# Delta rule's key and query norms in four column groups, and both windowed attentions in a new order with the band mask in the bias product

## The chip, the cores and the metric

The kernel runs on one core of a Trainium2 chip, as one launch. Its five engines (TensorE, VectorE, ScalarE, GpSimd, and SyncE for transfers) each run an instruction stream of their own and wait for one another on semaphores. The metric is the device time of a launch in microseconds.

## The reference

Two transformer blocks of different kinds follow each other, at a width of 1024, for 256 tokens (and 256 context tokens in the first block). Everything is float32. The first block has two layers, a gated delta rule mixer and a windowed attention; the second has, side by side, a convolution, a state space branch and another windowed attention, then a cross attention and an MLP. What the change touches, cut:

```python
def _l2_normalize(x):                       # first layer: queries and keys, 8 heads of 128
    return x * lax.rsqrt(jnp.sum(x * x, axis=-1, keepdims=True) + EPS)
qkv = jax.nn.silu(_short_conv(h @ w_in[:, :3072], conv_w))      # 512 tokens, 24 tiles of 128 channels
...
def _sink_softmax(logits, sink):            # both attentions: a further logit without a value
    return softmax(concatenate([sink, logits], -1), -1)[..., 1:]
# first attention: 16 heads of 64, 4 for keys and values; 256 queries;
# 512 keys (256 of the context, 256 latent ones within +-128), masked with a window
p = _sink_softmax(concatenate([q @ kc.T, where(allowed, q @ kb.T, -inf)], -1), sink)
ox = p[..., :256] @ vc + p[..., 256:] @ vb
...
# second attention: 16 heads of 64; each block of 128 queries sees its own and the previous 128 keys
bias = rel_table[bucket[dist]]              # by distance, 32 buckets, one value per head
logits = where((dist >= 0) & (dist < 128), q @ k.T * 64 ** -0.5 + bias, -1e30)
...
h = causal_depthwise_conv(a * sigmoid(gate), w, b)              # second block, 31 taps, 1024 channels
```

## The kernel before

The order of the work is written out by hand: each engine has a program, a sequence of calls such as `delta_pe`, `window_heads_dve` or `feed_pool`, and steps are named. `k.AC.after(st, "sq", m)` is the semaphore and the count at which ScalarE has done step `sq` number m of stage `st`; `mark` counts it. Nothing is reordered afterwards.

**Weights.** All weights come as one stream of 554 units of eight 128x128 tiles (512 KB) through SyncE's queue. ScalarE rounds a unit to `weights_hi` (L214), GpSimd writes the remainder `weights_lo` (L224), and each product is three matmuls (L231 to L233), high by low, low by high and high by high. Most of TensorE's work is this; it runs weights as the stationary operand (8 tiles in depth) against 256 or 512 tokens.

**Delta projection** (`delta_pe` L649, `delta_act`, `delta_dve` L755). 33 tiles of 128 channels by 512 tokens go through `linear`: tile 0 holds the gates, tiles 1 to 24 q, k and v, tiles 25 to 32 z. `linear` calls `beside(n)` behind tile n, which places small matmuls between the tiles. For each q and k tile, VectorE does the short convolution from the bank (L743 and after), ScalarE the silu and a square into `k.sq`, and TensorE, behind tiles 3 to 18, sums the square over its 128 channels: four matmuls with the square as the stationary operand (128 tokens each) and one moving column of ones, into bank 4, columns 4m to 4m+3. When the sixteen sums are there ScalarE takes the root of 128x64 (L728) and VectorE the reciprocal (L786). Behind tiles 25 to 32 TensorE spreads two of the sixteen tiles' inverse norms over all partitions, each in four transposes of a broadcast column (L688), into banks 5 and 6, and VectorE multiplies q and k by them (L790).

**Windowed attention heads** (`window_heads_pe` L1533, `_act` L1576, `_dve` L1604), the same three functions for both attentions. A step n has two heads (hh) of two blocks of 128 queries (b), so four combinations x = 2b + hh. The first attention has 512 keys for all of them, the second 128 for b = 0 and 256 for b = 1. Per step TensorE does the four score products (banks 0 to 3), then, for the step before, transposes of the probabilities in turns with the outputs (L1544 and L1555): `turned(1)`, `output(0)`, `turned(2)`, `output(1)` and so on. An output is a chain of matmuls over the key tiles with 64 columns of v as the stationary operand. The two heads go to the two halves of the output's partitions, so hh selects one of two column halves of TensorE. VectorE adds the mask and takes the maximum with one custom instruction (L1621; ahead of it a memset of a column, and behind it a negation of the maximum), ScalarE takes the exponential with its sum, VectorE adds the sink's part (L1633), takes the reciprocal and multiplies (L1640), and ScalarE copies the transposed probabilities to `swa_pt` or `attn_pt` (L1585).

**Mask and bias of the second attention.** `rel_table` (32 buckets x 16 heads) times `bucket` (32 x 384 distances) gives the bias by distance (`band_pe`); it goes to DRAM and comes back skewed into `biasm`, 128 x 16 x 256. GpSimd then adds the band mask `band` to it in four additions of 1024 columns (`band_pool` L1762). In GpSimd's program they stand between the last unit of the first attention's query weights and its output's weights.

**Convolution.** `long_conv` (L1675) is a generator of single taps on VectorE; `take(conv, n)` does n of them. Channel tiles 0 to 3 are done before the second attention's projection, tile 4 (`CONV_APART`) within its heads, four taps per step in SBUF, and tiles 5 to 7 behind them. The others accumulate in banks 6 and 7, which the heads use for outputs.

## Time and profile before

| | |
|---|---|
| median of three runs | 2959.94 us (2954.56, 2959.94, 2963.52) |
| profiled execution | 2956.96 us, of it 2955.0 us span |
| granted clock of TensorE, mean | 0.981 of full speed |
| TensorE matmul | 2811.4 us busy, 95% of the span, 21638 instructions |
| TensorE weight load | 2427.7 us, 82% |
| GpSimd | 1543.2 us, 52% |
| VectorE | 1540.9 us, 52% |
| ScalarE | 1186.2 us, 40% |
| chain that ended last | TensorE 82%, VectorE 8%, GpSimd 3%, ScalarE 3%, issue 2%, DMA 1% |

Busy time is the union of the instructions' intervals on an engine. The chain is followed back from the last instruction to what released each one, so its shares tell which engine the end of the program hung on, and where. The difference between the execution's time and its span, 1.96 us, lies outside the profiled instructions. The page gives averages over the whole program; the changed code lies in three stretches of it, and what these look like is read from the trace.

### The profile page before, as it was taken

Reading aid. Unit: us, or ns where it says so; the run is one execution under the profiler, and the core shown is the slowest. Engines: PE = TensorE matmul, PEld = TensorE weight load, DVE = VectorE, ACT = ScalarE, POOL = GpSimd, SP = SyncE. Lnnn points to the kernel's source line nnn. Section 1 sums busy time; section 2 is a strip of 40 time slices with the busy share of each in tenths; the row PEclk is TensorE's granted clock in tenths of the full one; section 3 lists DMA queues with packets and bytes.
Section 4 is the critical chain, followed back from the end, with each engine's and each line's share of the span. In section 5 each row is a group of like instructions: output and inputs, shape, how many; then the busy total and the mean of one; then the engine's idle time right before and its main releaser. Section 6 shows DMA issues by size and latency. Waiting matters only on the chain.

```text
span 2955.0 us, 52281 instructions
## 1 busy us (share of the span) xinstructions
PE 2811.4 (95%) x21638; PEld 2427.7 (82%) x21638; DVE 1540.9 (52%) x2922; ACT 1186.2 (40%) x2076; POOL 1543.2 (52%) x861
## 2 busy tenths in 40 slices
PE   7999999988889999999999998999998998998999
PEld 5888878877777788887888885799997898997999
DVE  4777235535554667316665136554284865723570
ACT  4222234324453322223222244544445465544553
POOL 4444453343324544444444452388884565696697
PEclk9999999999999999999999998999998999999999
DMA  6555322210001555324554225155553343354365
GB/s 256 203 198 200 99 76 82 89 58 3 4 3 51 174 176 178 128 93 144 178 182 156 93 89 100 57 195 190 173 186 101 109 142 108 108 164 136 116 199 164
DMA packets 106123, 381.05 MB, mean 129 GB/s; under 512 B 11392, under 2 KB 16800, under 8 KB 104608
## 3 DMA queue, kind: packets, MB, share of 16 engines
q1 hardware_dynamic: 87456, 310.60, 32.2%
q10 hardware_dynamic: 18432, 67.12, 6.5%
q8 instruction: 172, 2.82, 0.4%
q14 instruction: 63, 0.52, 0.1%
HBM read 373.47 MB, written 4.19 MB: 128 GB/s over the span
## 4 chain that ended last, share of the span: by engine, by line
PE 82%; DVE 8%; POOL 3%; ACT 3%; issue 2%; DMA 1%; SPq 0%; ACTq 0%; DVEq 0%
PE bank L231 23%; PE bank L232 22%; PE bank L233 22%; POOL weights_lo L224 2%; PE bank L822 2%; DVE norm_work L504 1%; PE upper_banks L1555 1%; DVE norm_work L498 1%; PE upper_banks L231 1%; PE upper_banks L232 1%; PE upper_banks L233 1%; DMA ada_first<-w_ada 1%; DVE square_sums L451 1%; PE bank L919 1%; PE upper_banks L838 1%
## 5 line engine op out<-in xcount | busy, mean ns | idle before, releaser
L224 POOL TENSOR_TENSOR weights_lo<-weights_landing,weights_hi 128x1024 fp32r<-128x1024 f32 x554 | 1338.5, 2423 | 1101.0 <-ACT weights_hi L214 1100.4
L214 ACT ACTIVATE weights_hi<-weights_landing 128x1024 fp32r<-128x1024 f32 x554 | 586.5, 1061 | 1235.2 <-PE bank L233 1112.7
L231 PE MATMUL bank<-normed_hi,weights_lo 128*128 128x512 f32 (+1 forms) x2664 | 912.2, 342 | 17.6 <-POOL normed_lo L520 11.9
L232 PE MATMUL bank<-normed_lo,weights_hi 128*128 128x512 f32 (+1 forms) x2664 | 900.9, 338 | 0.0
L233 PE MATMUL bank<-normed_hi,weights_hi 128*128 128x512 f32 (+1 forms) x2664 | 900.0, 338 | 0.0
L231 PEld LDWEIGHTS bank<-normed_hi,weights_lo 128*128 128x128 f32 x2664 | 502.3, 189 | 95.2 <-POOL normed_lo L520 27.6
L233 PEld LDWEIGHTS bank<-normed_hi,weights_hi 128*128 128x128 f32 x2664 | 502.1, 188 | 61.6
L232 PEld LDWEIGHTS bank<-normed_lo,weights_hi 128*128 128x128 f32 x2664 | 502.6, 189 | 58.4
L231 PE MATMUL bank<-hidden_hi,weights_lo 128*128 128x512 f32 (+1 forms) x960 | 329.1, 343 | 0.0
L232 PE MATMUL bank<-hidden_lo,weights_hi 128*128 128x512 f32 (+1 forms) x960 | 329.1, 343 | 0.0
L233 PE MATMUL bank<-hidden_hi,weights_hi 128*128 128x512 f32 (+1 forms) x960 | 329.1, 343 | 0.0
L572 DVE TENSOR_TENSOR hidden_lo<-silus,hidden_hi 128x512 fp32r<-128x512 f32 (+1 forms) x88 | 210.9, 2397 | 87.3 <-ACT hidden_hi L559 87.3
L625 DVE SCALAR_TENSOR_TENSOR residual<-bank,gate,residual 128x256 f32<-128x256 f32 x80 | 35.5, 479 | 358.3 <-PE bank L233 358.3
L231 PEld LDWEIGHTS bank<-hidden_hi,weights_lo 128*128 128x128 f32 x960 | 180.1, 188 | 24.3
L232 PEld LDWEIGHTS bank<-hidden_lo,weights_hi 128*128 128x128 f32 x960 | 180.1, 188 | 24.2
L233 PEld LDWEIGHTS bank<-hidden_hi,weights_hi 128*128 128x128 f32 x960 | 180.1, 188 | 24.2
L390 DVE CUSTOM_DVE_ANT_0 ada_products<-ada_rows,upper_banks,k_cond_pack 128x1024 f32<-128x1024 f32 x128 | 163.3, 1276 | 22.9 <-DMA ada_rows<-w_ada_rows 14.0
L390 DVE CUSTOM_DVE_ANT_0 ada_rows<-ada_rows,upper_banks,k_cond_pack 128x1024 f32<-128x1024 f32 x128 | 163.1, 1274 | 0.0
L570 DVE TENSOR_TENSOR silus<-silus,bank 128x512 f32<-128x512 f32 (+1 forms) x88 | 54.7, 621 | 183.7 <-PE bank L233 158.7
L520 POOL TENSOR_TENSOR normed_lo<-norm_work,normed_hi 128x512 fp32r<-128x512 f32 (+1 forms) x72 | 76.6, 1068 | 75.1 <-DVE norm_work L504 75.1
L1689 DVE SCALAR_TENSOR_TENSOR upper_banks<-gl,k_pack,upper_banks 128x255 f32<-128x255 f32 (+14 forms) x210 | 99.3, 473 | 7.4
L451 DVE TENSOR_TENSOR square_sums<-square_sums,squares 128x512 f32<-128x512 f32 (+1 forms) x48 | 67.3, 1402 | 35.9 <-ACT squares L443 35.9
(447 smaller groups left out, 3912.1 us busy)
## 6 DMA issues: line engine op xcount, KB each, us to landing
weights_landing<-w_up SPq DMA_DIRECT2D x176, 512.0 KB, 3.5
ada_rows<-w_ada_rows ACTq DMA_DIRECT2D x128, 512.0 KB, 4.3
weights_landing<-w_down SPq DMA_DIRECT2D x88, 512.0 KB, 3.4
weights_landing<-w_dn SPq DMA_DIRECT2D x33, 512.0 KB, 3.4
weights_landing<-w_mlp_up SPq DMA_DIRECT2D x32, 512.0 KB, 3.4
weights_landing<-w_mlp_down SPq DMA_DIRECT2D x32, 512.0 KB, 3.5
weights_landing<-w_gate SPq DMA_DIRECT2D x24, 512.0 KB, 3.4
weights_landing<-w_xbc SPq DMA_DIRECT2D x24, 512.0 KB, 3.5
```

The costliest lines, as they stand in the source:

```text
L214: k.nc.scalar.activation(k.WH[:, u % SLOTS, :], k.W[:, u % LANDS, :], ACT.Copy).then_inc(*k.AC.mark(("unit hi", u)))
L224: k.nc.gpsimd.tensor_tensor(k.WL[:, u % SLOTS, :], k.W[:, u % LANDS, :], k.WH[:, u % SLOTS, :].bitcast(F32), ALU.subtract).then_inc(*k.PO. ...
L231: nc.tensor.matmul(out, ll, rh, start=start, stop=False, skip_group_check=True)
L232: nc.tensor.matmul(out, lh, rl, start=False, stop=False, skip_group_check=True)
L233: return nc.tensor.matmul(out, lh, rh, start=False, stop=stop, skip_group_check=True)
L390: nc.vector.tensor_tensor_reduce(k.row[r % ROW_LANDS][:] if c else k.row_out[:], k.row[r % ROW_LANDS][:], k.upper[:, c * D:(c + 1) * D], 1 ...
L451: k.nc.vector.tensor_tensor(s, s, k.sq[:, d % 2, 0:tokens], ALU.add).then_inc(*k.DV.mark((st, "sum", d)))
L520: k.nc.gpsimd.tensor_tensor(lo(d), work(d), hi(d).bitcast(F32), ALU.subtract).then_inc(*k.PO.mark((st, "lo", d)))
L570: nc.vector.tensor_tensor(s, s, k.B[(2 * p + 1) % 4][:, 0:tokens], ALU.mult).then_inc(*k.DV.mark((st, "raw", p)))
L572: nc.vector.tensor_tensor(lo(p), s, hi(p).bitcast(F32), ALU.subtract).then_inc(*k.DV.mark((st, "lo", p)))
L822: mm = k.nc.tensor.matmul(bank[block(to), at + c * BLK:at + (c + 1) * BLK], lhs(rows, to, c), rhs(rows, to, c), start=True, stop=True)
L1689: nc.vector.scalar_tensor_tensor(y[:, a:LAT], x[:, 0:LAT - a], w[:, at, j:j + 1], y[:, a:LAT], ALU.mult, ALU.add).then_inc(*k.DV.mark(("co ...
```

## The change

**Norms of the delta rule.** ScalarE writes the squares of four tiles into `sq4`. Behind tiles 6, 10, 14 and 18 TensorE sums four of them at once: four matmuls with 32 columns of ones as the stationary operand and 512 moving columns, one into each group of 32 output partitions (`block(j)`) of bank 4. ScalarE copies the bank to `norms`, and later takes four roots of 512 columns; VectorE takes four reciprocals of 512. The inverse norms now lie along the columns, so a spread is one matmul with 32 rows of the identity, and behind tiles 28 to 31 four of these go to banks 4 to 7. VectorE multiplies four q or k tiles per spread group.

**Heads.** The three functions are rewritten for both attentions. TensorE takes a block's two heads together: transposes of both, then scores of a later step, then the outputs, in which the two heads alternate from matmul to matmul. The maximum is taken as a minimum of the negated values (scale -1.0, with the sink negated once), so the memset and the negation are gone, and the exponential has scale -1.0. VectorE takes the first two maxima of step n+1 ahead of and between the multiplications of step n.

**Mask.** The mask is a 33rd row of `bucket` with a row of ones in `rel_table`; GpSimd's additions and the transfer of `band` are gone. VectorE waits for the skewed transfer itself.

**Convolution.** Tile 4 is now done during the second attention's projection, three taps per step and two at the last ones, in bank 7, and is copied out like the others.

```diff
     def beside(n):
-        m = n - 3
-        if 0 <= m < 16:
-            pe.wait_ge(*k.AC.after(st, "sq", m))
-            for c in range(CHUNKS):
-                mm = nc.tensor.matmul(k.B[4][:, m * 4 + c:m * 4 + c + 1], k.sq[:, m % 2, c * P:(c + 1) * P], k.C["ones"][:, 0:1],
...
+        g = (n - 6) // 4
+        if n >= 6 and n % 4 == 2 and g < 4:
+            pe.wait_ge(*k.AC.after(st, "sq", 4 * g + 3))
+            if g:
+                pe.wait_ge(*k.AC.after(st, "norms", g - 1))
+            for j in range(4):
+                mm = nc.tensor.matmul(k.B[4][block(j), :], k.C["ones"][:, 0:BLK], k.sq4[:, j, :], start=True, stop=True)
...
-        if n > QKV:
...
-                for c in range(CHUNKS):
-                    mm = nc.tensor.transpose(ck(k.B[bank], c), column(k.rr, m * 4 + c).to_broadcast([P, P]), k.C["ident"])
+        g = n - QKV - 4
+        if 0 <= g < 4:
+            pe.wait_ge(*k.DV.after(st, "r", g))
+            if g:
+                pe.wait_ge(*k.DV.after(st, "normed", 4 * g - 1))
+            for j in range(4):
+                pick = k.C["ident"][block(j), j * BLK:j * BLK + 1].to_broadcast([BLK, P])
+                mm = nc.tensor.matmul(k.B[4 + j][:], pick, k.norms[block(j), g, :], start=True, stop=True)
...
+            if m >= 7 and m % 4 == 3 and m < 20:
+                act.wait_ge(*k.PE.after(st, "stat", m // 4 - 1))
+                nc.scalar.activation(k.norms[:, m // 4 - 1, :], B[4][:], ACT.Copy).then_inc(*k.AC.mark((st, "norms", m // 4 - 1)))
...
+                for g in range(4):
+                    nc.scalar.activation(k.norms[:, g, :], k.norms[:, g, :], ACT.Sqrt, bias=k.C["eps"]).then_inc(*k.AC.mark((st, "rms", g)))
...
+            for g in range(4):
+                dve.wait_ge(*k.AC.after(st, "rms", g))
+                nc.vector.reciprocal(k.norms[:, g, :], k.norms[:, g, :]).then_inc(*k.DV.mark((st, "r", g)))
...
-    def output(n, x):
...
         for t in range(kt):
-            mm = nc.tensor.matmul(half(k.B[6 + n % 2], hh)[:, blk(b)], w.v[:, a // P + t, at:at + HEAD], w.pt[:, x, blk(t)],
+            for hh in range(2):
+                at = (2 * (n // 4) + hh) * HEAD
+                mm = nc.tensor.matmul(half(k.B[6 + n % 2], hh)[:, blk(b)], w.v[:, a // P + t, at:at + HEAD], w.pt[:, 2 * b + hh, blk(t)],
...
+    for n in range(KT):
+        turned(n, 0)
+        turned(n, 1)
+        scores(n + 1, 1)
+        outputs(n, 0)
+        turned(n, 2)
+        turned(n, 3)
+        scores(n + 2, 0)
+        outputs(n, 1)
...
-                nc.vector.memset(w.cols[:, p, 7, x:x + 1], 0.0).then_inc(*k.DV.mark((st, "scored", n, x)))
...
-                nc.vector.tensor_scalar(nm[p][:, x:x + 1], mx[p][:, x:x + 1], -1.0, None, ALU.mult).then_inc(*k.DV.mark((st, "nm", n, x)))
...
+        maximum(n, 2)
+        maximum(n, 3)
...
+        maximum(n + 1, 0)
...
+        share(n, 0)
+        share(n, 1)
+        maximum(n + 1, 1)
+        share(n, 2)
+        share(n, 3)
...
-def band_pool(k, pool):
-    pool.wait_ge(k.skewed, 32)
...
-    window_project_dve(k, dve, attn)
-    dve.wait_ge(*k.PO.after("band", "masked", 3))
-    window_heads_dve(k, dve, attn, band_mask(k), lambda n: take(conv, 4))
+    window_project_dve(k, dve, attn, lambda n: take(conv, 3 if n < KT + 2 else 2))
+    dve.wait_ge(k.skewed, 32)
+    window_heads_dve(k, dve, attn, band_mask(k))
...
-    t["late_bucket"] = (np.arange(32)[:, None] == bucket[None, :]).astype(f)
+    t["late_bucket"] = np.concatenate([(np.arange(32)[:, None] == bucket[None, :]).astype(f), band[None, :]])
```

On TensorE's queue, one step of the first attention's heads, before (L1566 is a score, L1544 a transpose, L1555 an output matmul; in the sizes 64x128 means that 64 output partitions are written, and x4 that four of the kind follow one another):

```order
L1566 MATMUL bank<-swa_k,swa_q 128x512 x4
L1544 MATMUL upper_banks<-k_cond_pack,swa_scores 128x128 x8
L1555 MATMUL upper_banks<-swa_pt,swa_v 64x128 x4
L1544 MATMUL upper_banks<-k_cond_pack,swa_scores 128x128 x4
L1555 MATMUL upper_banks<-swa_pt,swa_v 64x128 x4
L1544 MATMUL upper_banks<-k_cond_pack,swa_scores 128x128 x4
L1555 MATMUL upper_banks<-swa_pt,swa_v 64x128 x8
```

and after (L1564 is the transpose, L1555 now the score, L1579 the output):

```order
L1564 MATMUL upper_banks<-k_cond_pack,swa_scores 128x128 x8
L1555 MATMUL bank<-swa_k,swa_q 128x512 x2
L1579 MATMUL upper_banks<-swa_pt,swa_v 64x128 x8
L1564 MATMUL upper_banks<-k_cond_pack,swa_scores 128x128 x8
L1555 MATMUL bank<-swa_k,swa_q 128x512 x2
L1579 MATMUL upper_banks<-swa_pt,swa_v 64x128 x8
```

The scores now stand in pairs between the transposes and the outputs of another step, and the outputs come in eights, whose matmuls alternate between the column halves.

On VectorE's queue, from the last statistics of the second attention's projection to its first maximum, before (L1485 is the reciprocal of a norm, L1489 the normalising, L1620 the memset, L1621 the maximum and its read, L1625 the negation):

```order
L1485 RECIPROCAL rr<-rms 128x4
L1489 SCALAR_TENSOR_TENSOR attn_q<-attn_q,k_pack,upper_banks 128x256 x2
L1620 MEMSET attn_cols 128x1
L1621 ISA attn_scores,attn_cols<-bank,biasm,k_pack 128x128
L1621 ISA attn_cols 128x1
```

and after (L1746 is a tap of the convolution, L1750 its copy):

```order
L1491 RECIPROCAL rr<-rms 128x4
L1495 SCALAR_TENSOR_TENSOR attn_q<-attn_q,k_pack,upper_banks 128x256
L1746 SCALAR_TENSOR_TENSOR upper_banks<-gl,k_pack,upper_banks 128x232
L1746 SCALAR_TENSOR_TENSOR upper_banks<-gl,k_pack,upper_banks 128x231
L1746 SCALAR_TENSOR_TENSOR upper_banks<-gl,k_pack,upper_banks 128x230
L1495 SCALAR_TENSOR_TENSOR attn_q<-attn_q,k_pack,upper_banks 128x256
L1746 SCALAR_TENSOR_TENSOR upper_banks<-gl,k_pack,upper_banks 128x229
L1746 SCALAR_TENSOR_TENSOR upper_banks<-gl,k_pack,upper_banks 128x228
L1746 SCALAR_TENSOR_TENSOR upper_banks<-gl,k_pack,upper_banks 128x227
L1746 SCALAR_TENSOR_TENSOR upper_banks<-gl,k_pack,upper_banks 128x226
L1750 COPY cv<-upper_banks 128x256
L1659 ISA attn_scores,attn_cols<-bank,biasm,k_pack 128x128
```

The taps of channel tile 4 now stand around the last two normalisings and ahead of the first maximum, where there were none.

## Rows read from the trace of the kernel before

A row of the timeline is the start in us, the busy time of the group in us, engine, line, operation, output, inputs, sizes and count, and in brackets the idle time ahead of it with what ended it. PE is TensorE, PEld its weight load, DVE VectorE, ACT ScalarE, POOL GpSimd. A row of busy time by stretch is start and end in us, the length, then the busy time (and the instructions) of PE, PEld, DVE, ACT and POOL, the granted clock, the share of the DMA engines and GB/s.

**Rows 1.** Busy time by stretch; columns named ahead.
```profile
434.00:640.00 206.00, 202.72 (x984) 166.27 (x984) 103.76 (x151) 80.52 (x104) 82.80 (x38) 1.00 0.27 88
2262.00:2316.00 54.00, 41.78 (x227) 25.80 (x226) 46.96 (x226) 27.52 (x112) 0.00 (x0) 0.81 0.03 11
```

**Rows 2.** Timeline, VectorE, first tap of three tiles, 545 to 560 us.
```profile
545.82 0.75 DVE L743 TENSOR_SCALAR dn_convs<-bank,k_pack 128x512 f32<-128x512 f32 x1 [2.61 <-PE bank L233]
552.31 0.75 DVE L743 TENSOR_SCALAR dn_convs<-bank,k_pack 128x512 f32<-128x512 f32 x1 [2.61 <-PE bank L233]
557.91 0.75 DVE L743 TENSOR_SCALAR dn_convs<-bank,k_pack 128x512 f32<-128x512 f32 x1 [1.72 <-PE bank L233]
```

**Rows 3.** Timeline, end of the delta projection, 585 to 640 us.
```profile
587.13 1.09 PE L688 MATMUL upper_banks<-k_cond_pack,rr 128*128 128x128 f32 x8 [1.26 <-DVE rr L786]
...
613.71 1.29 DVE L790 SCALAR_TENSOR_TENSOR dn_qkv<-dn_qkv,upper_banks 128x512 f32<-128x512 f32 x2 [5.19 <-PE upper_banks L688]
620.18 1.29 DVE L790 SCALAR_TENSOR_TENSOR dn_qkv<-dn_qkv,upper_banks 128x512 f32<-128x512 f32 x2 [5.19 <-PE upper_banks L688]
```

**Rows 4.** Timeline, TensorE's column groups, and VectorE's 64-column reciprocal.
```profile
24.58 1.07 PE L297 MATMUL upper_banks<-ada_first,cond 128*32 128x256 f32 x16
...
586.52 0.55 DVE L786 RECIPROCAL rr<-rms 128x64 f32<-128x64 f32 x1 [2.33 <-ACT rms L728]
...
1783.54 0.42 PEld L1356 LDWEIGHTS upper_banks<-k_cond_pack,rr 128*64 128x64 f32 x8
```

**Rows 5.** Timeline, VectorE, the sums of pairs 0, 1, 2 and 7.
```profile
1800.69 0.16 DVE L1633 TENSOR_TENSOR swa_cols<-swa_cols 128x4 f32<-128x4 f32 x1 [0.78 <-ACT swa_cols L1596]
...
1809.50 0.16 DVE L1633 TENSOR_TENSOR swa_cols<-swa_cols 128x4 f32<-128x4 f32 x1 [3.06 <-ACT swa_cols L1596]
...
1817.99 0.17 DVE L1633 TENSOR_TENSOR swa_cols<-swa_cols 128x4 f32<-128x4 f32 x1 [1.17 <-ACT swa_cols L1596]
...
1868.72 0.16 DVE L1633 TENSOR_TENSOR swa_cols<-swa_cols 128x4 f32<-128x4 f32 x1 [1.16 <-ACT swa_cols L1596]
```

**Rows 6.** Timeline, GpSimd and VectorE, 1825 to 1838 us.
```profile
1825.95 9.61 POOL L1765 TENSOR_TENSOR biasm<-biasm,band 128x1024 f32<-128x1024 f32 x4 [39.10 <-DMA biasm<-skew]
1828.57 7.68 DVE L1640 TENSOR_SCALAR swa_scores<-swa_scores,swa_cols 128x512 f32<-128x512 f32 x4
```

**Rows 7.** Timeline, first attention's heads, pair 0 and pair 7.
```profile
1801.10 1.68 DVE L1640 TENSOR_SCALAR swa_scores<-swa_scores,swa_cols 128x512 f32<-128x512 f32 x4
...
1862.08 1.99 PE L1566 MATMUL bank<-swa_k,swa_q 64*128 64x512 f32 x8
...
1863.25 0.75 DVE L1621 CUSTOM_DVE_ANT_0 swa_scores<-bank,window,k_pack 128x512 f32<-128x512 f32 x1 [0.92 <-issue]
...
1864.22 0.72 ACT L1593 ACTIVATE swa_scores<-swa_scores,swa_cols 128x512 f32<-128x512 f32 x1 [1.65 <-DVE swa_cols L1620]
...
1864.94 0.58 ACT L1585 ACTIVATE swa_pt<-upper_banks 128x512 f32<-128x512 f32 x1
...
1865.57 0.85 PEld L1555 LDWEIGHTS upper_banks<-swa_pt,swa_v 128*64 128x64 f32 x8 [0.72 <-ACT swa_pt L1585]
...
1866.59 0.66 PE L1544 MATMUL upper_banks<-k_cond_pack,swa_scores 128*128 128x128 f32 x4
```

**Rows 8.** Timeline, VectorE and TensorE, second attention's heads.
```profile
2259.61 0.18 DVE L1485 RECIPROCAL rr<-rms 128x4 f32<-128x4 f32 x1 [3.38 <-ACT rms L1453]
...
2263.05 0.35 DVE L1621 CUSTOM_DVE_ANT_0 attn_scores<-bank,biasm,k_pack 128x128 f32<-128x128 f32 x1
...
2267.27 0.15 DVE L1633 TENSOR_TENSOR attn_cols<-attn_cols 128x4 f32<-128x4 f32 x1
...
2302.55 1.94 DVE L1689 SCALAR_TENSOR_TENSOR cv<-gl,k_pack,cv 128x232 f32<-128x232 f32 x4
...
2309.98 0.16 DVE L1633 TENSOR_TENSOR attn_cols<-attn_cols 128x4 f32<-128x4 f32 x1
...
2314.01 0.39 PE L231 MATMUL bank<-normed_hi,weights_lo 128*128 128x256 f32 x1
```

223 lines of the change are left out of this document (118 added, 105 removed).

## Prediction

> **What bounds the kernel now.** The profiled execution has a span of 2955.0 us and took 2956.96 us; the median of the three runs, 2959.94 us, is 2.98 us above it, within their own spread of 9 us. I read the page first (TensorE 95% busy and 82% of the chain that ended last), so an edit is worth what it takes from TensorE's queue, or from the ring of waits that TensorE hangs in where it is not full. The changed code runs in three stretches, and busy time by stretch tells them apart. In the delta projection (434 to 640 us) TensorE is busy for 202.7 of 206 us at full clock: matmuls in its queue are the price there. In the second block's attention heads (2262 to 2316) VectorE is busy for 47.0 of 54 us and TensorE for 41.8, at a mean granted clock of 0.81, so part of it at 1.2 instead of 2.4 GHz [rows 1]. The first attention's heads (1794 to 1877) are a ring over three engines. Then I read starts of repeated instructions in the timeline, since their spacing says what an iteration costs.
>
> **Delta sums.** VectorE's first tap starts once per tile: 6.49 us apart with a sum between the tiles, 5.60 us without [rows 2]. A sum is thus 0.89 us, and 16 go: 14.2 us. With a spread the spacing is 6.47, so 0.87 more than 5.60; eight go: 7.0. TensorE's 1.26 us wait for the reciprocal goes too, since the first spread now comes three tiles later [rows 3]. Removed: 22.5.
>
> Added are four groups of four matmuls with 32 stationary columns each (sums, four column groups) and four of four with 32 rows each (spreads, four row groups), all of 512 columns. The nearest row is the first block's modulation: four column groups, two rounds of 256 columns, sixteen records in 1.07 us [rows 4]. One round of 512 is the same stream. For the other end, the four score matmuls of 512 columns take 1.99 us, two row groups at a time [rows 7], so about 0.86 us each alone and 3.4 for a group of four that doesn't overlap. I take 1.07, the row with the same four groups: 8 x 1.07 = 8.6 (up to 27.5). Net 22.5 - 8.6 = **13.9 us**.
>
> What is added elsewhere lies under this. ScalarE gets four copies and three more square roots of about 0.6 us (a 512-column copy is 0.58 [rows 7]); it is busy for 80.5 of the stretch's 206 us [rows 1]. VectorE gets four reciprocals of 512 columns instead of one of 64 at 0.55 us [rows 4]; by columns that is at most 4.4 us each, 17.6 together. They start where the small one starts, and the spreads that need them are behind four, five, six and seven tiles, 22 to 39 us later. Without that cover each would be on the path in full. The multiplications follow in fours, 2.7 us against a tile of 5.6, and the last four are covered by tile 32.
>
> **The mask in the bias product.** The four GpSimd additions lie at 1825.95 to 1835.56, and in just that stretch VectorE's four multiplications take 7.68 us [rows 6], against 1.68 for the same four in the first pair [rows 7]. From sum to sum the pairs take 8.49 us undisturbed (1809.50 to 1817.99), but the seven steps from 1800.69 to 1868.72 take 68.03, which is 8.6 more than 7 x 8.49 [rows 5]. With the additions gone that 8.6 goes (6.0 in the multiplications, the rest around them and in TensorE's lower clock behind the stall). Next late is the ring itself.
>
> **The first attention's ring.** The new order is: scores of the next pair's block 0, its row maximum, the sum of this pair, shares, the next maximum, exponential, two copies, outputs, transposes, scores again. By rows 7: scores to maximum 1.17 (1862.08 to 1863.25); maximum 0.84 (0.75, and the read of its result estimated at 0.09); sum to first share 0.41 (1800.69 to 1801.10); two shares 0.84 (half of 1.68); maximum to exponential 0.87 (1863.25 to 1864.22 is 0.97; 0.22 of it lie behind the 0.75 and hold a negation that goes, estimated at 0.10); exponential 0.72; first copy 0.50 of its 0.58; second copy to outputs 0.63 (1864.94 to 1865.57); outputs; eight transposes 1.1 (four are 0.66 with the tail). All but the outputs: 7.08. The outputs of a block are sixteen records. In one column half eight take 0.85 of loading [rows 7]; the spread of the norms has the same shape, 64 columns with 128 moving, in alternating halves, and loads eight in 0.42 [rows 4]. So sixteen take 0.85 plus 0.15 to change over, 1.0, against 1.77 in one half. The ring is 8.08 us against 8.49, because the new order puts the outputs ahead of the next transposes: the interleaving gives little, and without the overlap it would be 8.85 and worse than now. Seven steps: 7 x 8.08 = 56.6 instead of 68.03, so 11.5 less; the last pair's outputs, 4 x 0.85 = 3.4 us on the path, halve: 1.6 less. The start up to the first sum stays. Together **13.1 us**.
>
> One page speaks against this term: the Trainium skill, "TensorE: Matmul & The Clock Gate", section "Packing small matmuls", says that a weight load overlaps matmuls in flight only where their row groups differ, and both halves here use all rows. The 0.42 beside 0.85 contradicts it for this shape; by the page the ring would be 8.85, the first rival.
>
> **The second attention's heads.** VectorE fills them. From the first sum (2267.27) to the last (2309.98) are seven steps of 6.10 us, each with four taps of the convolution, 1.94 us [rows 8]. Taps, memsets and negations gone (1.94 + 4 x 0.10), VectorE needs about 3.8 us. The ring of the same terms, with blocks of 128 and 256 columns, is between 4.1 at full clock and 5.2 with TensorE's three terms doubled at 1.2 GHz. I take 4.6, since the mean clock was between the levels. That is 7 x 1.5 = 10.5 less, and 0.2 less in the last outputs. Against it, the taps move into the projection: 32 at 0.5 us, three a tile, where VectorE idles 3.4 us before each tile's statistics. But from 2259.61 on there are eleven taps, 5.5 us, and VectorE's own 1.7 us of statistics and normalising, so the first maximum starts at 2266.8 instead of 2263.05, 3.7 us late, of which 1.9 (the first four taps, ahead of the first sum) are given back. Then 10.7 - 1.8 = 8.9; less 0.4 for a cold start behind the longer gap: **8.5 us**. The remaining three convolutions start when the heads end, as now, so they shift with them.
>
> **Sum.** 13.9 + 13.1 + 8.5 = 35.5. Span 2955.0 - 35.5 = 2919.5; with the 1.96 around it 2921.5; against the median it would be 2924.4. I forecast 2922.
>
> **Rivals.**
> 1. *Groups don't overlap.* The four-group sums and the outputs cost as much as one by one: 4 x (3.4 - 1.07) = 9.4 for the sums, 7 x 0.77 + 1.6 = 7.0 in the first heads, about 2 in the second: gain 17, time 2940. For it: nothing in the trace has 512 columns on four column groups. Against: the modulation and the norm spreads overlap [rows 4].
> 2. *Cold heads.* VectorE and ScalarE pace the heads, TensorE idles in small gaps and is granted 1.2 GHz throughout. Scores, outputs and transposes add 2.7 us to each ring in the first (19), and 5.6 instead of 4.6 in the second (7): gain 9.5, time 2947. For it: the 0.81. Against: TensorE has some 6.3 us of work in each 8.1.
> 3. *Shorter rings.* If TensorE is always ahead, ScalarE's queue closes the ring: sum to share 0.41, shares 0.84, 0.87 to the exponential, three exponentials 2.16, four copies 1.96, the output's copy 0.3 and 0.23 back to the sum make 6.8 us. That is 7 x 1.3 = 9 more, and 3.5 more at 4.1 in the second heads: 2909.
> 4. *The stall isn't GpSimd's.* Then 8.6 stays: 2930.
> 5. *Slower: a drain at every alternation.* The new matmuls change column half on every one. If each record then ran as long as an isolated one, about 0.27 us, a block's outputs would be 16 x 0.27 = 4.3 us, TensorE would have 8.6 + 4.3 for transposes and scores in each pair, 12.9 instead of 8.08: 7 x 4.8 + 3.3 = 37 us; the second heads add 7 and the delta groups 4. Then 48 - 35.5 = 12.5 slower, 2969. It decides from about 0.2 us per record. Against it stand the eight records loaded in 0.42 [rows 4], 0.05 each. A rule of the Trainium skill points this way, "TensorEngine Tiling (Array Packing)", section "Key Properties": changing the tiling mode drains the engine; but it excepts changing the tile, and the trace agrees with the exception for these shapes.
>
> **Chances.** Forecast (2912 to 2934) 0.60; rival 1 0.12; rival 2 0.08; rival 3 0.12; rival 4 0.04; rival 5 0.04. Range: 2905 (rival 3 and a little of what I don't see) to 2943 (rival 1 and its neighbourhood), which leaves out rivals 2 and 5, and a remainder. About 0.3%, 8.9 us, is what a measurement tells from no change, so faster means below 2951: 0.90 (all but rival 5 and the worse half of rival 2); same 0.06; slower 0.04.
>
> **What would show it.** Tiles 5.60 us apart except for one gap of about 1.1 us in four; a wait of TensorE at the first spread would say that the reciprocals aren't covered. No multiplication of VectorE of over 1 us in the first heads. Sums 8.1 us apart there and 4.6 in the second; 8.9 or more means no overlap in the outputs; below 7.5 means my ring isn't closed by TensorE. The first maximum of the second heads 3.7 us later against the last statistics than before. The forecast is wrong most easily in the rings: each 0.5 us in one is 3.5 us of time.

## The result, and the profile after

The changed kernel takes 2923.84 us in the median of four runs (2922.53 to 2930.22), the kernel before 2959.51 in its four; the ratio is 0.9885, with a 95% interval from 0.9864 to 0.9905. The forecast was 2922, within 2905 to 2943. The profiled execution took 2923.75 us, with a span of 2921.6 against 2955.0: 33.4 us less. In a later set six more runs gave a median of 2926.55 (2919.73 to 2930.95), ratio 0.9895 (0.9878 to 0.9911).

The page of the changed kernel, its span and the busy time of each engine:

```profile
span 2921.6 us, 51936 instructions
PE 2781.6 (95%) x21510; PEld 2393.9 (82%) x21510; DVE 1533.2 (52%) x2800; ACT 1188.2 (41%) x2083; POOL 1532.1 (52%) x857
```

Such shares say almost nothing of where the time went: TensorE is 95% busy in both. The starts of the same instructions in both timelines do. I took seven places in the program and the time between each two, in us:

| stretch | before | after | gained |
|---|---|---|---|
| start to the convolution of the second delta tile | 441.37 | 442.54 | -1.17 |
| from there to the first solve of the delta rule's heads | 203.40 | 190.35 | 13.05 |
| to the first maximum of the first attention | 1151.39 | 1151.81 | -0.42 |
| to the first matmul of its output projection | 80.72 | 65.82 | 14.90 |
| to the last statistics of the second attention's projection | 382.75 | 381.21 | 1.54 |
| to the first matmul behind its heads | 54.38 | 45.84 | 8.54 |
| to the first decay sums of the state space branch | 87.76 | 90.90 | -3.14 |
| to the end | 553.2 | 553.1 | 0.1 |

The prediction had 13.9, 13.1 and 8.5. The first two are as forecast within 2 us; the third came out to the tenth, and then 3.1 us of it were given back in a stretch whose instructions the change doesn't touch.

**Delta projection.** VectorE's timeline of the changed kernel, the first tap of three tiles, then the reciprocals; and TensorE's, a group of sums and the first group of spreads:

```profile
537.15 0.75 DVE L747 TENSOR_SCALAR dn_convs<-bank,k_pack 128x512 f32<-128x512 f32 x1 [1.72 <-PE bank L234]
543.93 0.75 DVE L747 TENSOR_SCALAR dn_convs<-bank,k_pack 128x512 f32<-128x512 f32 x1 [2.90 <-PE bank L234]
549.53 0.75 DVE L747 TENSOR_SCALAR dn_convs<-bank,k_pack 128x512 f32<-128x512 f32 x1 [1.72 <-PE bank L234]
...
578.55 12.99 DVE L791 RECIPROCAL dn_norms<-dn_norms 128x512 f32<-128x512 f32 x4 [2.74 <-ACT dn_norms L732]
```

```profile
513.45 1.07 PE L667 MATMUL upper_banks<-dn_squares,k_cond_pack 128*32 128x512 f32 x8
...
594.22 1.14 PE L688 MATMUL upper_banks<-dn_norms,k_cond_pack 32*128 32x512 f32 x8
```

The tiles are 5.60 us apart, and 6.78 where a group of sums stands between them, against 6.49 behind each of sixteen tiles before [rows 2]: a group costs 1.18. The spread groups start 6.87, 6.86 and 6.86 apart, so 1.26 each, with no wait ahead of the first, where there was one of 1.26 us [rows 3]. The four reciprocals take 3.25 us each and end at 591.5, under the tiles: the first group of spreads starts 15.7 us behind their start.

**First attention.** One step of its heads in the changed kernel, VectorE's and TensorE's timeline (L1659 is the maximum, L1687 the sum, L1666 the multiplications by the reciprocal; L1555 scores, L1564 transposes, L1579 outputs). A float32 matmul leaves two records in the timeline and a transpose one, so x16 is the eight output matmuls of a block:

```profile
1811.92 0.75 DVE L1659 CUSTOM_DVE_ANT_0 swa_scores<-bank,window,k_pack 128x512 f32<-128x512 f32 x1 [2.04 <-PE bank L1555]
1812.60 0.16 DVE L1687 TENSOR_TENSOR swa_cols<-swa_cols 128x4 f32<-128x4 f32 x1
1813.01 0.88 DVE L1666 TENSOR_SCALAR swa_scores<-swa_scores,swa_cols 128x512 f32<-128x512 f32 x2
1813.80 0.75 DVE L1659 CUSTOM_DVE_ANT_0 swa_scores<-bank,window,k_pack 128x512 f32<-128x512 f32 x1
```

```profile
1813.55 1.09 PE L1564 MATMUL upper_banks<-k_cond_pack,swa_scores 128*128 128x128 f32 x8
1814.57 1.13 PE L1555 MATMUL bank<-swa_k,swa_q 64*128 64x512 f32 x4
1816.52 1.09 PE L1579 MATMUL upper_banks<-swa_pt,swa_v 128*64 128x128 f32 x16 [0.82 <-DVE swa_cols L1659]
1817.55 1.09 PE L1564 MATMUL upper_banks<-k_cond_pack,swa_scores 128*128 128x128 f32 x8
1818.57 1.13 PE L1555 MATMUL bank<-swa_k,swa_q 64*128 64x512 f32 x4
```

From sum to sum it is 7.81 us, against 8.49 undisturbed [rows 5] and 16.49 in the fourth step, in which GpSimd's additions lie. Its two sums in the kernel before:

```profile
1826.48 1.84 DVE L1633 TENSOR_TENSOR swa_cols<-swa_cols 128x4 f32<-128x4 f32 x1 [1.16 <-ACT swa_cols L1596]
1842.97 0.16 DVE L1633 TENSOR_TENSOR swa_cols<-swa_cols 128x4 f32<-128x4 f32 x1 [2.49 <-ACT swa_cols L1596]
```

Seven steps are 54.98 instead of 68.03. Sixteen output records take 1.03 us to the next transpose, where a block's outputs took 1.77 at the end of a pair. The wait of 0.82 ahead of them ends with ScalarE's second copy (1815.32 to 1816.38); the releaser named is one that was long done.

**Second attention.** VectorE's sums are 4.28 us apart in the steady part, but 10.62 in the first two steps. Busy time by stretch (columns as in [rows 1], the granted clock is the third from the end): first from TensorE's last statistics matmuls of the projection to the end of the heads, then 7.43 us of the projection behind them; of the kernel before, and of the changed one:

```profile
2259.63:2314.01 54.38, 41.58 (x229) 25.16 (x229) 46.75 (x227) 28.68 (x113) 1.44 (x1) 0.81 0.04 14
2314.01:2321.44 7.43, 7.43 (x64) 7.43 (x64) 6.44 (x14) 4.45 (x6) 2.73 (x2) 1.00 0.00 1
```

```profile
2231.73:2277.57 45.84, 34.00 (x228) 20.59 (x228) 32.54 (x143) 27.91 (x113) 1.44 (x1) 0.77 0.05 15
2277.57:2285.00 7.43, 7.43 (x53) 7.43 (x52) 6.44 (x14) 3.12 (x5) 1.67 (x1) 0.78 0.02 3
```

After the change TensorE enters the next projection at 1.2 GHz (0.78 in the mean of these 7.43 us, where it was 1.00): 53 matmuls instead of 64 in the same 7.43 us, 11 x 0.117 = 1.3 us, and later in the same stretch it has a little more of 1.2 GHz than before (a mean clock of 0.87 from 50 to 90 us behind the heads, before 0.91).

### The profile page after: what moved, and what is told of

It is laid out like the page before. It is cut to its first block, busy times and chain, and to the rows that moved or that the text cites. A ratio compares the mean times of both kernels' runs of the same rounds, so it can differ in the third digit from the quotient of the medians.

```text
span 2921.6 us, 51936 instructions
## 1 busy us (share of the span) xinstructions
PE 2781.6 (95%) x21510; PEld 2393.9 (82%) x21510; DVE 1533.2 (52%) x2800; ACT 1188.2 (41%) x2083; POOL 1532.1 (52%) x857
## 4 chain that ended last, share of the span: by engine, by line
PE 84%; DVE 6%; POOL 3%; ACT 3%; issue 2%; DMA 1%; SPq 0%; ACTq 0%; DVEq 0%
PE bank L232 23%; PE bank L233 23%; PE bank L234 23%; POOL weights_lo L225 2%; PE bank L828 1%; DVE norm_work L505 1%; PE upper_banks L232 1%; PE upper_banks L233 1%; PE upper_banks L234 1%; DVE norm_work L499 1%; DMA ada_first<-w_ada 1%; DVE square_sums L452 1%; PE upper_banks L1564 1%; PE bank L1555 1%; PE bank L925 1%
## 5 line engine op out<-in xcount | busy, mean ns | idle before, releaser
L626 DVE SCALAR_TENSOR_TENSOR residual<-bank,gate,residual 128x256 f32<-128x256 f32 x80 | 35.5, 479 | 358.4 <-PE bank L234 358.4
L1746 DVE SCALAR_TENSOR_TENSOR upper_banks<-gl,k_pack,upper_banks 128x255 f32<-128x255 f32 (+14 forms) x240 | 113.5, 473 | 8.2
```

The lines of the kernel that those rows point to most:

```text
L626: nc.vector.scalar_tensor_tensor(x, k.B[n % 4][:, a - first:b - first], gate(n, c), x, ALU.mult, ALU.add).then_inc(*k.DV.mark(*([(st, "ev" ...
L1746: nc.vector.scalar_tensor_tensor(y[:, a:LAT], x[:, 0:LAT - a], w[:, at, j:j + 1], y[:, a:LAT], ALU.mult, ALU.add).then_inc(*k.DV.mark(("co ...
```

## The experiments

The theory: the three terms of the prediction, independent of one another. The rivals are those of the prediction; after the first traces the clock of the second attention's heads became the main open point. The runs were made in three sets. Each had the kernel before beside it (medians 2960.41, 2958.14 and 2957.39 us), and each ratio is against that; times of different sets are compared by the stretches of their traces.

### The delta norms alone

The kernel before with the first part of the diff only (`delta_alone`).

> The kernel before with the four-group sums and spreads of the delta rule's norms alone; heads, mask and convolution as before. If the parts are independent: the same as in the changed kernel's trace, where the first work of the delta rule's heads came 13.05 us nearer to the second convolution tile than before, so about 2946.5 against 2959.5 of the kernel before. If the shorter projection only exposes a weight transfer or GpSimd's remainder later (GpSimd is 40% busy there), part comes back: 2950 to 2959.

Measured: 2943.48 us (2942.16 to 2946.48), the kernel before on this chip 2960.41, ratio 0.9946 (0.9925 to 0.9967). The stretch between the second convolution tile and the first solve took 190.35 us, to the hundredth what it takes in the changed kernel, and the heads of the first attention took 80.65 (80.72 before). This part doesn't depend on the others. By the medians the gain is 17, with an interval from 10 to 22; the trace says 13.05 for this stretch. The rest of the difference is spread over stretches that the edit doesn't touch.

### The mask alone

The kernel before with the mask in the bias product (`mask_alone`):

```diff
-    band_pool(k, pool)
...
-    dve.wait_ge(*k.PO.after("band", "masked", 3))
+    dve.wait_ge(k.skewed, 32)
```

> The kernel before with the mask as a 33rd row of the bias product and without GpSimd's four additions; all else as before. If the additions slow VectorE's multiplications (prediction): the multiplications of the fourth step take 1.7 us instead of 7.68, all seven steps of the first attention are about 8.5 apart, and the time is 8.6 lower, 2951. If the stall has another cause (rival 4): the step stays at 14 to 17 us and the time at 2959 to 2960.

Measured: 2948.98 us (ten runs, 2945.23 to 2953.6), ratio 0.9966 (0.9955 to 0.9976): 10 us, 7 to 13 with the interval. The sums of the first attention, VectorE's timeline of this kernel:

```profile
1808.41 0.16 DVE L1633 TENSOR_TENSOR swa_cols<-swa_cols 128x4 f32<-128x4 f32 x1 [3.05 <-ACT swa_cols L1596]
1818.25 0.16 DVE L1633 TENSOR_TENSOR swa_cols<-swa_cols 128x4 f32<-128x4 f32 x1 [1.17 <-ACT swa_cols L1596]
1826.73 0.16 DVE L1633 TENSOR_TENSOR swa_cols<-swa_cols 128x4 f32<-128x4 f32 x1 [1.16 <-ACT swa_cols L1596]
1835.22 0.16 DVE L1633 TENSOR_TENSOR swa_cols<-swa_cols 128x4 f32<-128x4 f32 x1 [1.17 <-ACT swa_cols L1596]
```

The step of 16.49 is gone: the third and fourth are 8.48 and 8.49 (the rows are the sums at the ends of steps 1 to 4), and every group of four multiplications takes 1.67 or 1.68. The stall was GpSimd's, and rival 4 falls. The stretch of the heads is 7.0 shorter, not 8.6, because the second step took 9.84 in this execution, with a mean granted clock of 0.92 where before it was 1.00.

### The mask back in the changed kernel

The changed kernel with GpSimd's four additions and the transfer of `band`, as before (`mask_back`).

> The changed kernel with the band mask put back as GpSimd's four additions (and its transfer), so the new order of the heads meets them. If their price is what they do to VectorE's multiplications, it is the same here: four multiplications and maxima 6 us slower, 6 to 9 us in all, 2930 to 2933. If VectorE's 2 us of idle time in each step of 7.81 take it up: 2925 to 2928.

Measured: 2929.89 us, but from 2920.26 to 2934.48, ratio 0.9888 (0.9855 to 0.992); against the changed kernel that decides nothing. The trace does, for the first attention: its heads took 70.10 us, 4.28 more than without the additions. GpSimd's additions, and VectorE beside them:

```profile
1814.32 9.73 POOL L1819 TENSOR_TENSOR biasm<-biasm,band 128x1024 f32<-128x1024 f32 x4 [39.10 <-DMA biasm<-skew]
```

```profile
1814.23 2.98 DVE L1666 TENSOR_SCALAR swa_scores<-swa_scores,swa_cols 128x512 f32<-128x512 f32 x2
1817.13 0.74 DVE L1659 CUSTOM_DVE_ANT_0 swa_scores<-bank,window,k_pack 128x512 f32<-128x512 f32 x1
...
1820.52 1.25 DVE L1687 TENSOR_TENSOR swa_cols<-swa_cols 128x4 f32<-128x4 f32 x1
```

Two multiplications take 2.98 instead of 0.88 and an addition of four columns 1.25 instead of 0.16, while the maxima, which read a bank of PSUM, keep their 0.74 and the reciprocal of four columns its 0.18. So it is an instruction that is held up, by its kind, and not VectorE as a whole. The second expectation comes nearer: the new order has 2 us of idle time on VectorE in each step, and takes up a part. But the same execution had the second attention's heads at another clock:

```profile
2237.25:2289.48 52.23, 43.78 (x229) 25.65 (x229) 32.08 (x143) 28.68 (x113) 1.44 (x1) 0.53 0.04 14
```

These heads are the changed kernel's to the instruction, but they take 52.23 us instead of 45.84, at a mean of 0.53 instead of 0.77: 1.2 GHz in all seven steps (5.42 each) instead of in the first two.

### Outputs one head after the other

The changed kernel (`heads_in_turn`):

```diff
-        for t in range(kt):
-            for hh in range(2):
-                at = (2 * (n // 4) + hh) * HEAD
+        for hh in range(2):
+            at = (2 * (n // 4) + hh) * HEAD
+            for t in range(kt):
```

> The changed kernel, but the outputs of the two heads of a block one after the other, not alternating: one column half, then the other. If the overlap of the column halves is what shortens the outputs: sixteen records take about 1.8 instead of 1.06 us, the ring of the first attention goes from 7.81 to about 8.55, its last step's two blocks cost 1.5 more, and the second attention some 0.35 a step where TensorE closes its ring: 7 x 0.75 + 1.5 + 2 = 9 slower than the changed kernel, 2932. If ScalarE's queue closes the ring (rival 3): nearly unchanged, 2924 to 2926.

Measured: 2933.79 us (2928.81 to 2935.74), ratio 0.9909 (0.9887 to 0.9932). The first attention took 70.48 us, 4.66 more: 3.24 in seven steps and 1.37 behind the last sum. The second took 52.29, but again at 1.2 GHz throughout, so the median says nothing of it. TensorE's weight loads in the first attention, in turn and (the changed kernel) alternating:

```profile
1816.90 1.34 PEld L1579 LDWEIGHTS upper_banks<-swa_pt,swa_v 128*64 128x64 f32 x16 [1.33 <-issue]
```

```profile
1816.49 0.88 PEld L1579 LDWEIGHTS upper_banks<-swa_pt,swa_v 128*64 128x64 f32 x16 [1.62 <-DVE swa_cols L1659]
```

Alternating halves load sixteen in 0.88 us. In turn it is 1.34, not the 1.70 to 1.77 that two halves one after the other would cost by the rows of before. The alternation is worth 0.46 us a block, not the 0.77 by which rival 1 was priced.

### The ring: copies ahead of the next exponential

The changed kernel, on ScalarE (`copies_first`):

```diff
         copy_p(n - 1, 0)
         copy_p(n - 1, 1)
+        if n:
+            exp(n, 1)
         out_high(n - 2)
...
         exp(n + 1, 0)
-        exp(n + 1, 1)
```

> The changed kernel, but ScalarE copies the transposed probabilities of a step's block 0 ahead of the next step's second exponential, in both attentions. By the account of the ring (sum, shares, the next maximum, exponential, copies, outputs, transposes, scores), the next maximum and the exponential fall out of it: TensorE's outputs start about 0.85 us earlier, and ScalarE's queue closes the ring at about 6.9 instead of 7.81. Then seven steps of the first attention are 6 us shorter (49 instead of 54.98); in the second attention, where the same wait of TensorE is only 0.26 us, 0 to 2. About 2917 at equal clocks. If the ring is closed elsewhere: 7.8 stays.

Measured: 2924.74 us (2921.08 to 2930.22), ratio 0.9888 (0.9874 to 0.9903). In the trace the first attention takes 61.83 us instead of 65.82, and a step 6.91 (sums at 1807.39 and 1814.30) instead of 7.81, as worked out. Seven steps are 51.04, not the expected 49: the first took 9.81, where the granted clock was 0.55 and 0.60 in its first 8 us. TensorE of this kernel no longer waits ahead of the outputs of block 0:

```profile
1816.27 1.13 PE L1555 MATMUL bank<-swa_k,swa_q 64*128 64x512 f32 x4
1817.33 1.09 PE L1579 MATMUL upper_banks<-swa_pt,swa_v 128*64 128x128 f32 x16
1818.36 1.09 PE L1564 MATMUL upper_banks<-k_cond_pack,swa_scores 128*128 128x128 f32 x8
```

Only what closes the ring now was wrong in the expectation: not ScalarE's queue but TensorE's, transposes, scores, outputs, transposes and scores in a row, and between the last scores and the next transposes 1.6 us of VectorE. The median is that of the changed kernel, though 4 us are gained there; this execution, too, had the second attention at 1.2 GHz (52.24).

### TensorE's gaps filled

Matmuls that nobody reads, in the changed kernel, where TensorE waits around the second attention's heads (`filled_gaps`; beside these, four of 256 columns in the end of the projection):

```diff
     scores(0, 1)
+    busy(4, 6)
     scores(1, 0)
+    busy(4, 6)
...
         scores(n + 1, 1)
+        busy(n == KT - 1)
         outputs(n, 0)
...
         scores(n + 2, 0)
+        busy(n >= KT - 2)
         outputs(n, 1)
```

> The changed kernel with matmuls that nobody reads in TensorE's waits at the end of the second attention's projection and at the start and end of its heads (15 of 256 columns; none in the seven steps' steady part but the last two). If the waits ahead of the heads let the granted clock fall to 1.2 GHz: it stays at 2.4, seven steps of 4.3 us (30.0 instead of 32.04), the end after the last sum 4.1 instead of 5.09, and the following projection starts at full clock (1 to 3 us back): 4 to 6 less than the changed kernel's profiled execution and 10 less than an execution with the heads at 1.2 GHz throughout; all runs near 2919. If not: the fillers only stand in the way, 2924 to 2930.

Measured: 2914.53 us (2912.53 to 2919.85), ratio 0.9858 (0.9842 to 0.9875). All its executions have a mean clock of 0.982 to 0.987, above all ten of the changed kernel (0.973 to 0.980). The heads and the stretch behind them:

```profile
2232.87:2275.53 42.66, 34.17 (x255) 21.54 (x255) 32.61 (x143) 27.44 (x113) 1.44 (x1) 1.00 0.05 16
2275.53:2282.96 7.43, 7.43 (x65) 7.43 (x64) 6.44 (x14) 4.45 (x6) 2.73 (x2) 1.00 0.01 3
```

2.4 GHz from the first step on, all seven steps 4.28 or 4.29, 3.98 behind the last sum instead of 5.09, and the state space branch's stretch back at 87.84 us. So both the 3.18 us of the heads and the 3.1 given back were the clock's. TensorE's idle times over 1 us in the changed kernel, from the last statistics to the first transposes:

```profile
2231.73 0.61 PE L1352 MATMUL upper_banks<-k_pack,squares 128*128 128x2 f32 x4 [1.22 <-ACT rms L1459]
2234.14 1.12 PE L1362 MATMUL upper_banks<-k_cond_pack,rr 128*64 128x128 f32 x8 [1.17 <-DVE attn_q L1495]
2238.56 0.97 PE L1555 MATMUL bank<-attn_k,attn_q 64*128 64x128 f32 x4 [1.73 <-DVE attn_cols L1659]
2241.20 0.69 PE L1564 MATMUL upper_banks<-k_cond_pack,attn_scores 128*128 128x128 f32 x2 [1.66 <-DVE attn_scores L1666]
```

The granted clock is 1.00 in the 2 us ahead of 2231.73, 0.81 in the 2 us behind it and 0.50 in the next 2, ahead of the first score; in the kernel before it fell there too (0.58 and 0.50 from 2261.63 to 2265.63). With the gaps filled it is 1.00 throughout. The fillers stand in all four gaps and at the end of the heads, so which of them is needed isn't shown.

Not all of the difference between the two profiled executions is the fillers'. The span is 10.9 us shorter than the changed kernel's; 6.2 of it lies in these two stretches, 5.8 in the last one, to the end, and 1.1 is lost ahead. The last stretch has the same instructions in both and took from 547.0 to 553.8 us in the profiled executions of all kernels; why is open. Against an execution whose clock doesn't come back in the heads the two stretches gain 12 to 14 us (the table in the last experiment).

### Spreads without cover

The changed kernel (`spreads_early`):

```diff
-        g = n - QKV - 4
+        g = n - QKV - 1
```

> The changed kernel with the delta rule's four spread groups behind tiles 25 to 28 instead of 28 to 31, so that the reciprocals (four of 3.25 us in the changed kernel's trace) have no cover. The first group waits some 4.4 us for its reciprocal; the second needs the first one's multiplications, which stand behind all four reciprocals in VectorE's queue, another 5 or so: 8 to 10 us slower than the changed kernel, 2933. If tiles cover them anyway: 2924.

Measured: 2941.1 us (2933.31 to 2943.06), ratio 0.9937 (0.9922 to 0.9952). The stretch took 201.61 us, 11.3 more. The first group waits for its reciprocal, the second for the first one's multiplications, which stand behind all four reciprocals:

```profile
580.63 2.09 PE L688 MATMUL upper_banks<-dn_norms,k_cond_pack 32*128 32x512 f32 x8 [4.47 <-DVE dn_norms L791]
592.68 1.28 PE L688 MATMUL upper_banks<-dn_norms,k_cond_pack 32*128 32x512 f32 x8 [2.33 <-DVE dn_qkv L796]
601.09 1.14 PE L688 MATMUL upper_banks<-dn_norms,k_cond_pack 32*128 32x512 f32 x8
```

The place of the spreads is worth 11 of the 13 us. The waits are 4.47 + 2.33 of it; in the matmuls after them the granted clock is 0.50 from 580 to 585 us and 0.80 to 0.86 from 585 to 600, where the changed kernel has 1.00 (the first group takes 2.09 instead of 1.14), which leaves about 4.5 for the lower clock.

### Sums one at a time

The changed kernel (`sums_singly`); ScalarE's copies of the bank to `norms` move with the sums, which the cut leaves out:

```diff
-            for j in range(4):
-                mm = nc.tensor.matmul(k.B[4][block(j), :], k.C["ones"][:, 0:BLK], k.sq4[:, j, :], start=True, stop=True)
-            mm.then_inc(*k.PE.mark((st, "stat", g)))
+            mm = nc.tensor.matmul(k.B[4][block(j), :], k.C["ones"][:, 0:BLK], k.sq4[:, j, :], start=True, stop=True)
+            if j == 3:
+                mm.then_inc(*k.PE.mark((st, "stat", g)))
...
```

> The changed kernel with the sixteen sums of squares one at a time behind tiles 3 to 18 (the same matmuls with 32 columns of ones and 512 moving columns, each alone between two tiles) instead of four together. If the four column groups run together (forecast): one alone costs about as much as a group of four, 0.9 to 1.2 us, so 16 x 1.0 - 4 x 1.19 = 10 to 13 us slower, 2935. If a group is only four in a row (rival 1): one alone costs 0.3, and the time stays within 1 us of 2924.

Measured: 2936.56 us (2932.87 to 2944.17), ratio 0.993 (0.9913 to 0.9947). The stretch took 204.25 us, 13.90 more. One sum alone, TensorE's timeline:

```profile
475.36 1.05 PE L666 MATMUL upper_banks<-dn_squares,k_cond_pack 128*32 128x512 f32 x2
```

1.05 us, and the tiles are 6.77 apart, so one costs 1.17 us and four together 1.18. The four column groups run fully side by side, also with 512 columns, and rival 1 falls for the sums.

### Alternation and convolution with the clock held

The outputs in turn, on top of the filled gaps (`in_turn_filled`):

> filled_gaps with the outputs of a block's two heads one after the other. With the clock of the second attention held, this shows what the alternation is worth there, which heads_in_turn could not (its heads ran at 1.2 GHz). First attention: 3.2 a span of seven steps and 1.4 at the end, as measured, 4.7 in all. Second attention: its ring passes through ScalarE's queue and TensorE waits 0.69 and 0.26 us in each step of 4.28; eight records of the second block cost 0.3 to 0.4 more, the four of the first nothing: at most 0.35 a step, 2.5, and 0.5 at the end. So 5 to 8 slower than filled_gaps, 2920 to 2922; 2919 if the waits absorb it.

Measured: 2920.96 us (2920.58 to 2921.94), ratio 0.9876 (0.9861 to 0.9892). The first attention takes 4.3 more than in filled_gaps, the second 42.64 against 42.66: nothing. There TensorE waits 0.69 and 0.26 us a step for ScalarE's copies, and the eight records of a block take 0.66 us in either order.

The four taps a step back in the second attention's heads, in SBUF as before, on top of the filled gaps, behind the next step's first maximum (`taps_back_filled`):

```diff
         maximum(n + 1, 0)
+        fill(n)
         dve.wait_ge(*k.AC.after(st, "es", n))
...
-    window_project_dve(k, dve, attn, lambda n: take(conv, 3 if n < KT + 2 else 2))
+    window_project_dve(k, dve, attn)
     dve.wait_ge(k.skewed, 32)
-    window_heads_dve(k, dve, attn, band_mask(k))
+    window_heads_dve(k, dve, attn, band_mask(k), lambda n: take(conv, 4))
```

> filled_gaps with the convolution's channel tile 4 back in the second attention's heads, four taps (1.94 us) a step on VectorE, none in the projection, as in the kernel before. VectorE is busy for about 3.3 of 4.28 us a step, so a step becomes 5.3 to 5.7: 7 to 10 us more in seven steps; the first maximum comes 2.9 us earlier against the last statistics, of which 1.9 goes to the first four taps. 6 to 8 slower than filled_gaps, 2921 to 2923. If the new order leaves VectorE room for them: 2912 to 2915.

Measured: 2932.3 us (2927.52 to 2935.62), ratio 0.9913 (0.9896 to 0.993), 18 more than filled_gaps. The heads take 59.13 us, more than the 54.38 of the kernel before, and a step up to 7.21:

```profile
2259.45 0.35 DVE L1670 CUSTOM_DVE_ANT_0 attn_scores<-bank,biasm,k_pack 128x128 f32<-128x128 f32 x1 [0.97 <-PE bank L1559]
2259.73 1.99 DVE L1756 SCALAR_TENSOR_TENSOR cv<-gl,k_pack,cv 128x244 f32<-128x244 f32 x4
2261.64 0.15 DVE L1699 TENSOR_TENSOR attn_cols<-attn_cols 128x4 f32<-128x4 f32 x1
```

The one step that ran at 2.4 GHz throughout, the first, took 5.84 us, close to the 5.3 to 5.7 expected, though not because VectorE was full: it was busy for 4.77 of it. The taps stand in the ring, between the next step's first maximum and the sum, and lengthen it by 1.56 of their 1.94 us. What the expectation left out is the clock: TensorE now waits up to 1.84 us for the multiplications, the granted clock falls to 0.75 in the second step and 0.55 in the third, and the steps take 6.90 to 7.21, where the changed kernel's at 1.2 GHz take 5.46. In this place of the new order the taps turn the change of the second attention into a loss. A place for them outside the ring wasn't tried.

### All of it in one, and the changed kernel again

The filled gaps, the copies first, fillers around the first attention's heads as well (in bank 7; `best`), and

```diff
-    window_project_dve(k, dve, attn, lambda n: take(conv, 3 if n < KT + 2 else 2))
+    window_project_dve(k, dve, attn, lambda n: take(conv, 4))
```

> What the experiments point to: filled_gaps, with the copies first (the ring of the first attention at 6.92 instead of 7.81), fillers in the first attention's waits too, and the taps of channel tile 4 four at a time, so that none stands behind the last statistics of the second attention's projection. First attention 6.2 less in seven steps and about 1.5 at its cold start; second attention: the first maximum 2 to 2.9 earlier. 9 to 11 less than filled_gaps: 2904. If the longer VectorE work in the projection delays its statistics (four taps, 2.0 us, into a wait of 2.0): 2907 or more.

Measured: 2913.94 us (2906.55 to 2916.4), ratio 0.9848 (0.983 to 0.9866). The edit of the taps was wrong: `take(conv, 4)` in all eleven steps is 44 taps, not 32. Twelve of channel tile 5 were taken too early, into a bank that the heads' outputs overwrite, so its convolution is not the reference's, and they stand just where none was meant to be, ahead of the first maximum. This kernel is no candidate, and of the second attention it says nothing. Of the first it does: 59.55 us, 6.3 less than the changed kernel, with 2.4 GHz from the start (1.00 in every window of 4 us from 1780 to 1796, where the changed kernel has 0.50 to 0.92).

The changed kernel again, on the same chip (`after_again`):

> The changed kernel once more, beside the version above on the same chip, and to see how many of its executions have the second attention's heads at 1.2 GHz throughout. If the clock there decides between two cases 6.4 us apart: times from 2920 to 2931, with the granted clock 0.973 in the long ones and 0.978 or more in the short ones.

Measured: 2926.55 us (2919.73 to 2930.95). The times rise roughly as the mean clock falls, but not in two groups: 2919.73, 2920.61, 2925.68, 2927.42, 2928.57 and 2930.95, at 0.977, 0.980, 0.978, 0.975, 0.975 and 0.974. Its profiled execution shows a third case: the heads took 48.25 us, with 27.02 us for five steps, 5.40 each, and then 4.28. So the clock comes back at different times in the heads, from after the second step to not at all.

How often, the profiles tell: seven profiled executions have the second attention's heads of the changed kernel with nothing filled (with the outputs in turn in `heads_in_turn`, with ScalarE's copies first in `copies_first`). Heads and the stretch behind them, to the first decay sums of the state space branch, in us:

| run | heads | stretch behind | together | clock back in the heads |
|---|---|---|---|---|
| changed kernel | 45.84 | 90.90 | 136.7 | after two steps |
| sums_singly | 45.76 | 91.02 | 136.8 | after two steps |
| after_again | 48.25 | 88.31 | 136.6 | after five |
| mask_back | 52.23 | 90.60 | 142.8 | not at all |
| heads_in_turn | 52.29 | 91.04 | 143.3 | not at all |
| copies_first | 52.24 | 91.31 | 143.6 | not at all |
| spreads_early | 52.24 | 92.12 | 144.4 | not at all |
| filled_gaps | 42.66 | 87.84 | 130.5 | never lost |

Where the clock came back late but stayed (after_again: 1.00 in the 7.43 us behind the heads) the next stretch took 2.6 us less, which makes up for the longer heads. A run's time depends by 6 to 8 us on when the clock comes back here; what decides that, no run shows.

## Why the prediction was right, point by point

- **Delta sums: right, 13.05 for 13.9.** What is removed was 22.5 as read. A group of sums costs 1.18 and one of spreads 1.26, not the 1.07 of the modulation: 4 x 1.18 + 4 x 1.26 = 9.8 for 8.6 (the stretch gained 0.3 more than these leave). The row with the same four groups was the right one to take, and the other end, 3.4, was far off, because four column groups cost what one costs (1.17).
- **Reciprocals under the tiles: right, with less cover than I wrote.** They take 3.25 us, below my bound of 4.4. The spreads that need them start 15.7 to 36.3 us behind the first one's start, not 22 to 39: I had counted a tile too many. "Without that cover each would be on the path in full" would be 13.0; the 11.3 measured are 6.8 of waits and some 4.5 of lower clock, so its size is near by luck.
- **The mask: right in cause, 8.6 for 7.0 to 8.3.** The long step became an ordinary one, 16.49 to 8.49, and one of 8.80 8.48, which is 8.3; the execution lost 1.35 of it to the clock in another step.
- **The first attention's ring: right, 7.81 for 8.08.** Its links are those named. Read off the step shown above: scores to maximum 1.16 for 1.17; maximum 0.68 for 0.84; sum to share 0.41; two shares 0.79 for 0.84; next maximum to exponential 0.79 for 0.87; exponential 0.73; first copy 0.49; then 0.70 for 0.63; outputs 1.03 for 1.0; transposes 1.02 for 1.1. The sum can start before the maximum's read has ended, which I had counted. The seven steps are 13.05 shorter for 11.5; the last pair is 1.2 for 1.6, and the way to the first sum, which I had left as it was, 0.6 shorter (3.90 for 4.53).
- **Rival 1, no overlap: false for both.** Its price was too high besides: the outputs in turn cost 4.7 in the first attention, not 7.0, and nothing in the second.
- **The Trainium skill's rule on weight loads: the measurement decides against it for this shape.** The Trainium skill, "TensorE: Matmul & The Clock Gate", section "Packing small matmuls", has loads overlap only across row groups. Here all rows are used, and alternating column halves load sixteen in 0.88 us, in turn in 1.34.
- **The second attention's heads: the sum was right (8.5), its terms were not.** I took 4.6 us a step as a mean between the levels; it is 4.28 at 2.4 GHz and 5.3 to 5.5 at 1.2, which is 4.58 with two cold steps, but 5.42 where the clock doesn't come back. The first maximum came 2.9 us later against the last statistics (6.34 for 3.42), not 3.7. Behind the last sum it took 5.09 where I had 3.8. Seven steps 10.7 less, the first sum 1.1 later and the end 1.1 longer make the 8.5. The cold start is no new cost either: the kernel before had one too. The step that failed is "less 0.4 for a cold start": the clock took 3.1 back in the next projection. In the profiled execution these gave 5.4 net for 8.5. Half of rival 2 is thus true, in some executions and for the second attention only (0 to 6.4 us), and the first attention's TensorE, with 6.4 us of work in 7.81, kept 2.4 GHz once its first step was over.
- **Why the total is within 2 us.** The span fell by 33.4 for 35.5: 0.9 less in the delta norms, 1.8 more in the first attention, and 3.1 less from the clock behind the second. The stretches that nothing touches moved by -1.17, -0.42 and +1.54, which cancel, and the profiled execution was one in which the clock came back early in the second attention; in one where it didn't, the same sum would have missed by 8. That is luck: of the seven in the table above, four kept 1.2 GHz throughout. The medians of the two sets, 2923.84 and 2926.55, are 2 and 5 us above the forecast.
- **Rival 3 was half true:** with one move on ScalarE the ring is 6.91, but TensorE closes it.
- **Rival 5, a drain at each alternation: false.** A block's eight output matmuls, each in the other half from the one before, take 1.03 us for their sixteen records, 0.06 a record, where the rival had 0.27.

The kernel with the filled gaps has the lowest median of all but the faulty one, 0.9858 of before (0.9842 to 0.9875) against 0.9885 (0.9864 to 0.9905) and 0.9895 (0.9878 to 0.9911) of the changed one in its two sets of runs, and that without any useful work added; they were not run side by side. With the copies first, and the gaps of the first attention filled as well, the traces promise 6 us more; that version wasn't run without the wrong taps.

## What to carry to other kernels

In a loop over several engines, list the links from one sum to the next and price each from a row: it gives the period to 4%, tells which edit shortens it (one instruction moved behind two others on ScalarE took 0.9 us off each step), and which one sits in it (four taps of 1.94 us lengthened it by 1.56 at full clock, with VectorE idle for 1.07 us of the step). A gain in short, waiting pieces of TensorE's work is only worth what the clock leaves of it: look at the granted clock ahead of, in and behind the stretch, in several executions, before believing one time. Four small float32 matmuls of 32 stationary and 512 moving columns, laid in separate column groups, cost what one does here (1.18 and 1.17 us).
